# Splitting three of four blocks of an expert's down product, and moving one conversion to ScalarE, in a mixture-of-experts stage on Trainium2

## What is computed

```python
gates = jnp.sum(jax.nn.one_hot(eidx, N_EXPERTS, dtype=jnp.float32) * wsel[..., None], axis=1)
...
for e in range(N_EXPERTS):            # w_gate, w_up: 1024 x 512; w_down: 512 x 1024; all float32
    he = jax.nn.silu(t @ w_gate[e]) * (t @ w_up[e])
    out = out + gates[:, e:e + 1] * (he @ w_down[e])
```

## Time and profile before

| | before |
|---|---|
| median of the runs | 896.84 us (895.25 to 897.25) |
| the profiled execution, its own time | 895.08 us |
| its span, first to last instruction | 893.3 us |
| busy: PE, VectorE, ScalarE, GpSimd | 87%, 61%, 45%, 10% |
| busy in one slot of the loop (19.4 us): PE, VectorE, ScalarE | 19.40, 13.71, 10.04 us |
| TensorE's granted clock, mean of the span | 0.951 of 2.4 GHz |

### The profile page before, as it was taken

One profiled execution on the slowest core, in us unless ns is written; L12 is line 12 of the kernel. 1 busy time (PEld: TensorE's weight loads), 2 busy tenths in 40 slices (PEclk: granted clock), 3 DMA queues, 4 the chain that ended last, 5 costly groups with the idle time before them and its releaser, 6 DMA issues.

```text
span 893.3 us, 12804 instructions
## 1 busy us (share of the span) xinstructions
PE 781.4 (87%) x4071; PEld 564.0 (63%) x4072; DVE 544.1 (61%) x664; ACT 401.6 (45%) x444; POOL 86.9 (10%) x143
## 2 busy tenths in 40 slices
PE   2799999999999996589950799999999999999982
PEld 0577787878778783368830566777666777666531
DVE  1467474555747554745678576777776677777317
ACT  5225463654655353822321445555544555544313
POOL 2000111102111120220004000000000000000043
PEclk9899999999999998599995799999999999999997
DMA  8928386594947746210047979758999999996483
GB/s 318 346 68 265 100 283 195 186 291 134 338 122 260 214 167 248 89 28 1 0 162 270 380 271 331 283 182 295 372 384 380 372 381 372 381 385 250 143 274 124
DMA packets 130055, 215.38 MB, mean 241 GB/s; under 512 B 4650, under 2 KB 55914, under 8 KB 130035
## 3 DMA queue, kind: packets, MB, share of 16 engines
q1 hardware_dynamic: 127156, 204.64, 66.0%
q0 software_dynamic: 2880, 10.49, 3.2%
HBM read 186.81 MB, written 45.09 MB: 260 GB/s over the span
## 4 chain that ended last, share of the span: by engine, by line
PE 78%; DVE 8%; DMA 6%; POOL 2%; issue 2%; SPq 1%; ACT 1%; POOLq 0%; DVEq 0%; ACTq 0%
PE z L860 44%; PE fill_ps L1523 17%; PE z L1523 10%; DMA ada_w<-in_ada_w 3%; PE fill_ps L1440 2%; PE z L961 2%; DVE exp_w L844 1%; SPq L1063 1%; PE fill_ps L1446 1%; PE fill_ps L984 1%; POOL slots_in L510 1%; DVE ew_sp L1369 1%; DMA w_pair<-in_sb_w_qkv 1%; DVE h_T L1288 1%; DMA slots_in<-h_tok,row_i 1%
## 5 line engine op out<-in xcount | busy, mean ns | idle before, releaser
L479 DVE TENSOR_TENSOR w_lo<-exp_w,w_hi 128x1024 fp32r<-128x1024 f32 x144 | 172.0, 1223 | 94.3 <-ACT w_hi L475 93.1
L475 ACT ACTIVATE w_hi<-exp_w 128x1024 fp32r (+1 forms) x144 | 151.4, 1061 | 91.7 <-PE z L860 87.9
L860 PE MATMUL z<-w_hi,x_slotT_hi 128*128 128x512 f32 x288 | 124.3, 432 | 5.9 <-DVE x_slotT_lo L770 5.9
L860 PE MATMUL z<-exp_w,hidT 128*128 x288 | 126.7, 593 | 1.4 <-DVE hidT L794 1.1
L860 PE MATMUL z<-w_hi,x_slotT_lo 128*128 128x512 f32 x288 | 115.6, 401 | 0.0
L860 PE MATMUL z<-w_lo,x_slotT_hi 128*128 128x512 f32 x288 | 114.8, 399 | 0.0
L860 PEld LDWEIGHTS z<-exp_w,hidT 128*128 128x128 f32 x288 | 54.4, 190 | 63.8 <-issue 62.3
L1523 PE MATMUL fill_ps<-h_hi,wp_hi 128*128 128x512 f32 x192 | 77.8, 405 | 1.6 <-DVE h_lo L1294 1.6
L1523 PE MATMUL fill_ps<-h_lo,wp_hi 128*128 128x512 f32 x192 | 76.7, 399 | 0.0
L1523 PE MATMUL fill_ps<-h_hi,wp_lo 128*128 128x512 f32 x192 | 76.0, 396 | 0.0
L592 ACT ACTIVATE y_slot<-z 128x1024 f32<-128x1024 f32 x18 | 18.5, 1025 | 113.3 <-PE z L860 113.3
(11 more groups left out here) (270 smaller groups left out, 1295.8 us busy)
## 6 DMA issues: line engine op xcount, KB each, us to landing
exp_w<-in_exp_w_gate SPq DMA_DIRECT2D x19, 2048.0 KB
exp_w<-in_exp_w_up SPq DMA_DIRECT2D x19, 2048.0 KB
exp_w<-in_exp_w_down SPq DMA_DIRECT2D x18, 2048.0 KB
ada_w<-in_ada_w SPq DMA_DIRECT2D x12, 2048.0 KB, 9.5
slots_in<-zeros SPq DMA_DIRECT2D x7, 2048.0 KB, 13.0
w_pair<-in_sb_w_qkv SPq DMA_DIRECT2D x24, 512.0 KB, 5.3
x_slot<-slots_in SPq DMA_DIRECT2D x18, 512.0 KB, 11.1
slots_out<-y_slot SPq DMA_DIRECT2D x18, 512.0 KB, 10.1
```

The lines of the kernel that those rows point to most:

```text
L475: act.activation(w_hi[:, u % RING, :].unsqueeze(1), raw_unit(b, u), ACT.Copy).then_inc(hi_ready, 1)
L479: dve.tensor_tensor(w_lo[:, u % RING, :].unsqueeze(1), raw_unit(b, u), w_hi[:, u % RING, :].bitcast(F32).unsqueeze(1), ALU.subtract).then_ ...
L860: return pe.matmul(out, lhsT, rhs, start=start, stop=stop, skip_group_check=True)
```

## The change

- Of each down product in the loop, blocks 0 to 2 of four are made in three passes from parts, block 3 in whole float32 as before (`split_out`). `hidT` becomes `hidT_hi` (ScalarE) and `hidT_lo` (VectorE) for these three blocks. The rings serve 11 units per slot in the loop instead of 8 (`WUNITS`, `units_before`).
- ScalarE makes the high parts of the down weights and of `hidT` (`last_down`) after the up half's, and the high part of the next inputs (`next_x_hi`), which VectorE made before, after that.
- On VectorE the order in an iteration becomes: up half's low parts, `hidT`, the gate product, low parts of down blocks 0 and 1, the hidden product, the next inputs' low part, low part of down block 2, four low parts of the next gate half.
- A partition now holds neighbouring rows of a weight (8 p + k, for down 4 p + k), so that each partition's load is one run of 16 KB; the turns pick every eighth (fourth) column to match.

```diff
--- before.py
+++ after.py
@@ -195,6 +195,7 @@
     slot_tab = sb("slot_tab", [P, TAB], I32)
     fetch_w = sb("fetch_w", [P, NE - 1])
     sq_tmp = sb("sq_tmp", [P, D])
+    tmp_at = next_place()
     tmp = sb("tmp", [P, D])
     phase_r = ExitStack()
     h2_tok = sb("h2_tok", [P, NT, D], c=phase_r)
@@ -212,12 +213,17 @@
     y_slot = sb("y_slot", [P, D])
     RING = 4
     UK = KD // RING
+    KS = 3
+    WUNITS = 2 * RING + KS
     w_lo = sb("w_lo", [P, RING, UK * FE], F32R)
     gate_diag = sb("gate_diag", [P, NT, 2, P])
     w_hi = nc.alloc_sbuf_tensor_at("w_hi", [P, RING, UK * FE], F32R, offset=h_T_at, align_bytes=32)
     y_rows = exp_w[:, 0, 0:NT * 2 * D].rearrange("p (t r n) -> p t r n", r=2, n=D)
     g_fin = exp_w[:, 1, 4096:4096 + D]
     g_ffn = tmp
+
+    hidT_hi = nc.alloc_sbuf_tensor_at("hidT_hi", [P, KS, P], F32R, offset=tmp_at, align_bytes=32)
+    hidT_lo = nc.alloc_sbuf_tensor_at("hidT_lo", [P, KS, P], F32R, offset=tmp_at + 4 * KS * P, align_bytes=32)
 
     ZIN = -(-(MAX_SLOTS + 1) // (NPAIR - 1))
     ZOUT = -(-(MAX_SLOTS - NE - 1) // (NPAIR - 1))
@@ -361,6 +367,7 @@
     sig_step = sem("sig_step")
     hid_ready = sem("hid_ready")
     hidT_mm = sem("hidT_mm")
+    hidT_hi_ready = sem("hidT_hi_ready")
     hidT_kept = sem("hidT_kept")
     down_ready = sem("down_ready")
     y_slot_kept = sem("y_slot_kept")
@@ -435,10 +442,10 @@
         fetch_over(1, 0, *first)
         with sp.Fori(1, m + 1) as j:
             before, now = next_of(j - 1), next_of(j)
-            sp.wait_ge(lo_ready, (2 * RING) * j + RING)
+            sp.wait_ge(lo_ready, units_before(j) + RING)
             fetch_over(0, j, *now)
             load_slot(j + 2)
-            sp.wait_ge(lo_ready, (2 * RING) * (j + 1))
+            sp.wait_ge(lo_ready, units_before(j) + 2 * RING)
             fetch_over(1, j, *now)
             sp.wait_ge(down_ready, j)
             sp.nop(nofuse=True)
@@ -463,8 +470,13 @@
 
         more = {} if cond is None else {"cond": cond}
         dst = exp_w[:, bass.ds(b, 1), i * 4096:(i + 1) * 4096].rearrange("p b (k f) -> p b k f", f=(FE, FE, D)[i])
-        src = io[("exp_w_gate", "exp_w_up", "exp_w_down")[i]][0].rearrange("e (k p) f -> p e k f", p=P)
+        src = io[("exp_w_gate", "exp_w_up", "exp_w_down")[i]][0].rearrange("e (p k) f -> p e k f", p=P)
         sp.dma_start(dst, src[:, bass.ds(e, 1)], **more).then_inc(exp_loaded[i], 16)
+
+    def units_before(j):
+
+
+        return 0 if isinstance(j, int) and j == 0 else j * WUNITS - KS
 
     def raw_unit(b, u):
 
@@ -572,17 +584,38 @@
             b = slot_expert(act, j) % 2
             act.wait_ge(exp_loaded[1], slot_fetched(act, j))
             for u in range(RING):
-                act.wait_ge(unit_used, (2 * RING) * j + u + 1)
+                act.wait_ge(unit_used, units_before(j) + u + 1)
                 hi_unit(act, b, RING + u)
-            act.wait_ge(unit_used, (2 * RING) * j + RING)
+            act.wait_ge(unit_used, units_before(j) + RING)
             act.activation(sig[:, :], zb(0), ACT.Sigmoid).then_inc(gate_sig, 1)
+
+        def last_down(j):
+
+            b = slot_expert(act, j - 1) % 2
+            act.wait_ge(exp_loaded[2], slot_fetched(act, j - 1))
+            act.wait_ge(hidT_mm, j)
+            act.activation(hidT_hi[:, :, :], fill_ps[:, 0, 0:KS * P].rearrange("p (k c) -> p k c", c=P),
+                           ACT.Copy).then_inc(hidT_hi_ready, 1)
+            for u in range(KS):
+                act.wait_ge(unit_used, units_before(j) + RING + u + 1)
+                hi_unit(act, b, 2 * RING + u)
+
+        def next_x_hi(j):
+
+            act.wait_ge(x_slotT_mm, j + 2)
+            act.wait_ge(unit_used, units_before(j) + 2 * RING)
+            act.activation(x_slotT_hi[:, :, :], z[:, 2048:3072].rearrange("p (k c) -> p k c", c=P),
+                           ACT.Copy).then_inc(x_hi_ready, 1)
 
         def next_gate(j):
 
             b = slot_expert(act, j + 1) % 2
             act.wait_ge(exp_loaded[0], slot_fetched(act, j + 1))
             for u in range(RING):
-                act.wait_ge(unit_used, (2 * RING) * j + RING + u + 1)
+                if isinstance(j, int):
+                    act.wait_ge(unit_used, RING + u + 1)
+                else:
+                    act.wait_ge(unit_used, units_before(j) + 2 * RING + min(u + 1, KS))
                 hi_unit(act, b, u)
 
         def keep_y(j):
@@ -592,11 +625,14 @@
             act.activation(y_slot[:, :], z[:, 1024:2048], ACT.Copy).then_inc(y_slot_kept, 1)
 
         this_up(0)
+        next_x_hi(0)
         next_gate(0)
         with act.Fori(1, m + 1) as j:
             act.wait_ge(table_set, j + 1)
             act.activation(zero_a[:, :], eps1[:, :], ACT.Sigmoid).then_inc(table_set, 1)
             this_up(j)
+            last_down(j)
+            next_x_hi(j)
             next_gate(j)
             keep_y(j - 1)
         act.wait_ge(table_set, m + 2)
@@ -763,9 +799,10 @@
         m = dve.value_load(slot_tab[0:1, TAB_N:TAB_N + 1], min_val=NE - 2, max_val=MAX_SLOTS - 2)
 
         def keep_slotT(j):
-            dve.wait_ge(x_slotT_mm, j + 1)
             rows_T = z[:, 2048:3072].rearrange("p (k c) -> p k c", c=P)
-            dve.tensor_copy(x_slotT_hi[:, :, :], rows_T).then_inc(x_hi_ready, 1)
+            if isinstance(j, int) and j == 0:
+                dve.wait_ge(x_slotT_mm, 1)
+                dve.tensor_copy(x_slotT_hi[:, :, :], rows_T).then_inc(x_hi_ready, 1)
             dve.wait_ge(x_hi_ready, j + 1)
             dve.tensor_tensor(x_slotT_lo[:, :, :], rows_T, x_slotT_hi[:, :, :].bitcast(F32),
                               ALU.subtract).then_inc(x_slotT_kept, 1)
@@ -785,8 +822,23 @@
 
             b = slot_expert(dve, j) % 2
             for u in us:
-                dve.wait_ge(hi_ready, (2 * RING) * j + RING + u + 1)
+                dve.wait_ge(hi_ready, units_before(j) + RING + u + 1)
                 lo_unit(dve, b, RING + u)
+
+        def rest_of_down(j, us):
+
+            b = slot_expert(dve, j - 1) % 2
+            for u in us:
+                dve.wait_ge(hi_ready, units_before(j) + 2 * RING + u + 1)
+                lo_unit(dve, b, 2 * RING + u)
+
+        def keep_split_hidT(j):
+
+            whole = fill_ps[:, 0, :].rearrange("p (k c) -> p k c", c=P)
+            dve.wait_ge(hidT_hi_ready, j + 1)
+            dve.tensor_copy(hidT[:, KS:KF, :], whole[:, KS:KF, :])
+            dve.tensor_tensor(hidT_lo[:, :, :], whole[:, 0:KS, :], hidT_hi[:, :, :].bitcast(F32),
+                              ALU.subtract).then_inc(hidT_kept, 1)
 
         def keep_hidT(j):
 
@@ -801,26 +853,30 @@
         def keep_hid(j):
 
             dve.wait_ge(sig_step, j + 1)
-            dve.wait_ge(unit_used, (2 * RING) * (j + 1))
+            dve.wait_ge(unit_used, units_before(j) + 2 * RING)
             dve.tensor_tensor(hid[:, :], sig[:, :], zb(1), ALU.mult).then_inc(hid_ready, 1)
 
-        def gated(j):
-
-            gate_by_sig(j)
-            b = slot_expert(dve, j + 1) % 2
+        def rest_of_gate(j):
+
+            b = slot_expert(dve, j) % 2
             for u in range(RING):
-                if u == RING // 2:
-                    keep_hid(j)
-                    keep_slotT(j + 1)
-                dve.wait_ge(hi_ready, (2 * RING) * (j + 1) + u + 1)
+                dve.wait_ge(hi_ready, units_before(j) + u + 1)
                 lo_unit(dve, b, u)
 
         rest_of_up(0)
-        gated(0)
+        gate_by_sig(0)
+        keep_hid(0)
+        keep_slotT(1)
+        rest_of_gate(1)
         with dve.Fori(1, m + 1) as j:
             rest_of_up(j)
-            keep_hidT(j - 1)
-            gated(j)
+            keep_split_hidT(j - 1)
+            gate_by_sig(j)
+            rest_of_down(j, range(2))
+            keep_hid(j)
+            keep_slotT(j + 1)
+            rest_of_down(j, range(2, KS))
+            rest_of_gate(j + 1)
         rest_of_up(m + 1, range(RING - 1))
         keep_hidT(m)
         rest_of_up(m + 1, range(RING - 1, RING))
@@ -958,7 +1014,8 @@
         def turn_slot(src):
 
             for k in range(KD):
-                mm = pe.transpose(z[:, 2048 + k * P:2048 + (k + 1) * P], src[:, k * P:(k + 1) * P], ident[:, :])
+                mm = pe.transpose(z[:, 2048 + k * P:2048 + (k + 1) * P], src[:, :].rearrange("p (c k) -> p k c", k=KD)[:, k, :],
+                                  ident[:, :])
             mm.then_inc(x_slotT_mm, 1)
 
         pe.wait_ge(x_slot_loaded, 16)
@@ -969,7 +1026,7 @@
         def half_in(j, i, us=range(RING)):
 
             for u in us:
-                pe.wait_ge(lo_ready, (2 * RING) * j + i * RING + u + 1)
+                pe.wait_ge(lo_ready, units_before(j) + i * RING + u + 1)
                 for k in range(UK * u, UK * (u + 1)):
                     cols = slice((k - UK * u) * FE, (k - UK * u + 1) * FE)
                     acc(zb(i), x_slotT_hi[:, k, :], w_hi[:, u, cols], start=(k == 0))
@@ -981,13 +1038,33 @@
 
             pe.wait_ge(hid_ready, j + 2)
             for k in range(KF):
```

(24 more changed lines are left out.)

## The result

The changed kernel takes 898.68 us in the median (895.84 to 900.51, 17 runs) beside 895.15 us (893.08 to 898.64, 17 runs) for the kernel before, measured beside it: a ratio of 1.0029, 95% interval 1.0019 to 1.0039. So it is slower, as forecast, by 0.29%, a little over the 0.2% that can be told (the interval begins at 0.19%); but by some 2.6 us (the ratio) to 3.5 us (the medians) where 5.9 was forecast. A second measurement of the same kernel gave 1.0033 (1.0017 to 1.0049). The profiled execution took 898.62 us, beside 895.08 for that of before.

The account below looks back on a forecast made before the run. PE alone was taken to bound the loop. Pause 1.28 less 0.95 given back adds 0.33 us a slot: 895.08 + 0.6 + 16 x 0.33 = 901 us (902.7 from the median); range 898 to 907, 8 in 10: 892 to 912.

Parts of the forecast that it names:

- What bounds it: In the loop, PE alone sets the beat, without pausing, in periods of 19.37 us.
- what the passes give: Down product on PE: 5.91 us against 6.86, giving back 0.95 a slot; PE's own work becomes 18.43.
- The engines' loads: Per slot, VectorE rises to about 16.2 us and ScalarE to about 14.7; neither bounds against PE's 18.4.
- The term that decides: Before down block 2, PE waits for VectorE's low part: chain 4.02 us, wanted at 2.80, pause 1.28 a slot.
- smaller pause: Chain to block 2 under 3.67 us, so the kernel is faster: 892.5 with half the pause, 882 without; chance 0.14.
- Strided turns at nothing: PE's twelve turns a slot, loaded at a step, cost nothing extra; upper bound 1.31 us a slot.
- the gift: The 0.95 us a slot that PE gives back in the down product through the three passes.
- Transfers at nothing: Weight loads in 16 KB runs change nothing, since nothing on the chain waits for them; cover 4.6 us.
- The third rival: 16 KB runs move weights 10% slower, transfers bind, a slot needs some 21.2 us: 913 us; chance 0.04.
- Prologue: PE's gap in slot 0 grows by a net 0.5 us, 0.6 in all with the clock.
- The sum: Whole execution: 895.08 + 0.6 + 16 x 0.33 = 901 us; from the median, 902.7.
- What would show it: Loop signs: right, sixteen pauses of 1.0 to 1.45 us and period 19.6 to 19.9; wrong, period under 19.3.

Follow-up runs that it names:

- d2_first: The changed kernel with the third split down block's low part moved on VectorE ahead of the hidden product and next inputs' low part; 883.52 us, ratio 0.9867.
- x_hi_dve: The changed kernel with the high part of the next inputs back on VectorE, ahead of their low part; 911.76 us, ratio 1.0183.
- d2_first_2k_pro: d2_first with the earlier kernel's loads and turns, and prologue gate parts put ahead of the inputs' parts on ScalarE and VectorE; 878.05 us, ratio 0.9809.
- four_blocks_2k_pro: d2_first_2k_pro with all four blocks of each down product in the loop made in three passes; 876.89 us, ratio 0.9787.

## Why the prediction was right on the sign and wrong on the size

- *What bounds it; what the passes give.* Right. Without a pause the period is 18.41, where 18.43 was summed.
- *The engines' loads.* Right: in the version without the pause VectorE was busy 16.14 and ScalarE 14.39 us of 18.40; 16.2 and 14.7 were forecast.
- *The term that decides.* The place, the cause and the count were right: one pause in each of 16 slots, ended by block 2's low part behind the inputs' low part. **The size of the pause was the step that failed: the hand-overs in its chain were priced too high.** The links summed to 4.02, and 3.67 was measured:

| link | forecast | measured | from |
|---|---|---|---|
| PE to ScalarE | 0.30 | 0.20 | 609.42 to 609.62 |
| inputs' high part | 1.04 | 1.03 | 609.62, line 607 |
| ScalarE to VectorE | 0.20 | 0.03 | 610.65 to 610.68 |
| inputs' low part to the next | 1.15 | 1.14 | 610.68 to 611.82 |
| block 2's low part, and to PE | 1.33 | 1.27 | 611.82 to 613.09 |

The durations held to 0.01. Of the 0.35 us, 0.27 are the two hand-overs whose price was taken from rows of ring parts, and with a register operation put at both the chain grew by 0.32. A further 0.06 is PE's hand-over: I took 0.10 where the prologue showed 0.15; with 1.23 for the low part it measured 0.04. The bounds were too narrow. The low end of the second hand-over, 0.15, was a ring row as well; that of the first, 0.27, was VectorE's (the hidden product, line 805), which is 0.27 in the changed kernel too (609.42 to 609.69) though its addresses are fixed, while ScalarE's is 0.20. And the bounds were not added up rightly: with the 0.10 to PE the lowest ends make 3.91 and not 3.80, the highest, with 0.15, make 4.11 and not 4.15, and the pause's lower bound of 1.00 leaves out the hold of 0.08. The hold itself measured 0.11. The pause was 0.98 instead of 1.28, next to the 0.95 given back. The rival "smaller pause" had its break-even at 3.67, and the chain came out just there: the loop is decided by hundredths.
- *Strided turns at nothing.* Off by 0.07 us a slot, 1.1 us over the loop; without it the periods of before and after are 19.37 and 19.38. So the sign was right in the loop by luck: the pause, which was to make it slower, cancels with the gift, and what is left of the loop's loss comes from a term that was put at nothing. The reasoning by the moving operand's rate was near; the upper bound of 1.31 was far off. The Trainium skill (Advanced Engine Details and Errata, section Memory Cachelines) says that an access which goes to a new 16-byte line each time pays a penalty. The trace agrees for the load itself, 195 ns instead of 141, and shows that eight turns in a row hide nearly all of it (0.114 us apart instead of 0.109).
- *Transfers at nothing.* Right on the chain. Packets fell from 130055 to 95240, the next inputs landed 4.3 to 11.2 us after their issue in the changed kernel, and no PE wait in the loop ends at a DMA. The third rival's bound is out: in d2_first, with runs of 16 KB and a period of 18.48, the queues moved 402 GB/s in a slot (679.00 to 697.40) and kept up; with the runs of before, at 18.41, 399.
- *Prologue.* Forecast +0.6, measured +1.5. The gap itself grew by 0.9 (3.32 to 4.24) and not by 0.5: I had the right late part, but left out ScalarE's register loads ahead of it, which idle the engine for 0.57 us, though I had priced such loads on VectorE. The other half is the stretch from the first turn to the next turns, with slot 0's gate half in it, 12.40 us before and 12.93 after, at a granted clock of 0.62 and 0.59, in which no instruction differs but the turns and the loads. These alone don't make it: x_hi_dve, with the loads and turns of the changed kernel, took 12.43 there at a clock of 0.62, and d2_first_2k_pro, with those of before, 12.88 at 0.60. In all twelve profiles the stretch follows the clock, from 12.30 at 0.63 to 12.96 at 0.59. So these runs don't show this half to be the change's; what follows it grew by 0.96 (17.60 to 18.56).
- *The sum.* 16 x 0.33 = 5.3 was 1.2 for the loop (4.1 too many); 0.6 was 1.5 for the prologue (0.9 too few). Together 2.7, within the 2.6 to 3.5 measured, though 0.5 of it goes with the clock and is not shown to be the change's; the 0.6 ahead of the first turn, which the profiles show too, belongs to no step and is as small as the profiles differ among themselves.
- *What would show it.* The period, 19.45, fell between the "right" of 19.6 to 19.9 and the "wrong" of under 19.3: the signs were set for the sum, and left out the middle in which a right mechanism has a smaller size.

## What to carry to other kernels

When a hand-over between engines is priced from a row, look at what the receiving instruction is: one with its address in a register had an operation of its own on the sequencer between the wait and the work, and its hand-over here was 0.14 to 0.18 us longer than that of the same instruction with a fixed address, for an operation of 0.10 to 0.13 us. When a change gives a busy engine less work, look for the instruction order on the engines that feed it: here one line in the wrong place ate all that the arithmetic had saved, and moving it up gave a kernel 1.3 to 1.4% faster than the one before. And where a sum is the difference of two terms near each other (0.95 against 1.28), a tenth in one link decides the sign, so the bounds of the links matter more than their best values.

## What the hardware showed beyond that

**The same code, the same pause, two clocks.** The two last kernels have the same prologue; PE idles 2.5 us in both and then runs the same 24 matmuls and four turns. Windows of that stretch, first d2_first_2k_pro:

```profile
512.85:515.53 2.68, 0.17 (x1) 0.00 (x1) 2.18 (x4) 2.13 (x3) 0.00 (x0) 1.00 1.02 408
515.53:521.66 6.13, 6.13 (x28) 4.99 (x29) 4.92 (x5) 3.37 (x5) 0.00 (x0) 1.00 1.04 393
```

and four_blocks_2k_pro:

```profile
512.24:514.92 2.68, 0.17 (x1) 0.00 (x0) 2.18 (x4) 2.12 (x3) 0.00 (x0) 1.00 1.03 411
514.92:522.60 7.68, 7.67 (x29) 6.15 (x30) 4.93 (x5) 3.37 (x5) 0.00 (x0) 0.78 1.04 393
```

The first stays at the granted clock of 1.00 (2.4 GHz); the second falls to the lower level for part of it, 0.78 in the mean, and takes 1.55 us longer for the same work. By finer windows its clock is still 1.00 through the pause and until 516.0, and 0.50 from 517.0 to 519.0: it falls more than 1 us after PE has taken up work again. What decides between the two, no run here shows. So a prologue's time here is known to no better than that from one profile. The 29.25 us of the second, whose clock there is that of before (0.78), is the fairer measure of the new order; the 28.15 of the first is 1.1 less (1.55 less here, and 0.45 more in the stretch ahead of it, 12.88 beside 12.43).
